# A recurrence in four chunks: the next chunk's inverse moved between this chunk's state products, with second buffers and banks of their own

## The reference

```
def step(state, inp):
    r_t, w_t, k_t, v_t, a_t, b_t = inp
    sa = jnp.einsum('bhvk,bhk->bhv', state, a_t)
    state = (state * w_t[:, :, None, :] + sa[..., None] * b_t[:, :, None, :]
             + v_t[..., None] * k_t[:, :, None, :])
    return state, jnp.einsum('bhvk,bhk->bhv', state, r_t)
```

## Time and profile before

| | |
|---|---|
| runs | 2697.29, 2707.37, 2708.58 us; median 2707.37 |
| profiled execution | 2712.13 us, of which the span of the instructions is 2710.4 |
| mean granted TensorE clock | 0.966 |
| recurrence, from 216.0 to 382.6 us | 166.6 us; TensorE busy 150.2, VectorE 66.5, ScalarE 35.4, clock 0.86 |

### The profile page before, as it was taken

How to read it: one execution, slowest core, us unless ns; L and a number is a source line. 1 busy time by engine, 2 the same in 40 slices (tenths; PEclk the granted TensorE clock), 3 DMA queues, 4 the chain that set the end, 5 groups by cost and what they waited for, 6 DMA issues and landing times.

```text
span 2710.4 us, 29623 instructions
## 1 busy us (share of the span) xinstructions
PE 2567.2 (95%) x12176; PEld 1986.1 (73%) x12176; DVE 1481.6 (55%) x1678; ACT 1133.3 (42%) x1329; POOL 155.1 (6%) x185
## 2 busy tenths in 40 slices
PE   6989989799999999899989999999999899999998
PEld 4667866587788887687757768888868566888876
DVE  3675343788888888546565543333354744333344
ACT  3422222577787777322334232222252644222223
POOL 1000001111110110000000100000100010000010
PEclk9888889899999999999989999999999999999999
DMA  6122321599999999422201222232312012222220
GB/s 255 61 77 103 110 78 62 209 359 366 362 357 359 360 354 341 160 79 97 86 20 63 80 84 84 80 109 76 118 63 93 32 43 75 80 99 105 69 99 31
DMA packets 64569, 388.77 MB, mean 143 GB/s; under 512 B 13361, under 2 KB 13489, under 8 KB 22577
## 3 DMA queue, kind: packets, MB, share of 16 engines
q1 hardware_dynamic: 53712, 373.20, 38.2%
q0 software_dynamic: 9280, 8.42, 0.9%
q10 hardware_dynamic: 1440, 5.24, 0.5%
HBM read 391.00 MB, written 20.97 MB: 152 GB/s over the span
## 4 chain that ended last, share of the span: by engine, by line
PE 81%; DVE 8%; ACT 4%; DMA 3%; issue 2%; POOL 0%; DVEq 0%; ACTq 0%; SPq 0%; POOLq 0%
PE psD L2696 67%; DMA ring<-w_moe 3%; PE psA L1984 1%; PE psA L2769 1%; DVE ring_r L935 1%; PE psA L2924 1%; DVE ring_r L2379 1%; ACT ring_r L2197 1%; ACT ring_r L733 1%; PE psA L2914 1%; PE psA L1054 1%; PE psD L1928 1%; PE psA L2015 1%; PE psA L2704 1%; PE psA L2749 1%
## 5 line engine op out<-in xcount | busy, mean ns | idle before, releaser
L2696 PE MATMUL psD<-rounded,ring_r 128*128 128x512 f32 (+1 forms) x6168 | 1454.9, 397 | 16.4 <-DVE ring_r L2379 12.6
L2696 PEld LDWEIGHTS psD<-rounded,ring_r 128*128 128x128 f32 (+1 forms) x6168 | 1155.6, 188 | 316.2 <-issue 22.5
L2379 DVE TENSOR_TENSOR ring_r<-ring,ring_r 128x2048 fp32r<-128x2048 f32 (+3 forms) x143 | 307.0, 2147 | 235.7 <-ACT ring_r L2197 232.0
L2696 PE MATMUL psD<-ring_r,rounded 128*128 128x512 f32 (+1 forms) x1728 | 411.0, 394 | 7.4 <-DVE ring_r L935 2.8
L2197 ACT ACTIVATE ring_r<-ring 128x2048 fp32r<-128x2048 f32 (+3 forms) x143 | 251.9, 1762 | 390.4 <-PE psD L2696 370.2
L2696 PEld LDWEIGHTS psD<-ring_r,rounded 128*128 128x128 f32 x1728 | 318.3, 190 | 89.1 <-issue 9.7
L935 DVE TENSOR_TENSOR ring_r<-ring,ring_r 128x2048 fp32r<-128x2048 f32 x128 | 293.1, 2291 | 47.2 <-ACT ring_r L733 45.9
L733 ACT ACTIVATE ring_r<-ring 128x2048 fp32r<-128x2048 f32 x128 | 245.2, 1917 | 59.3 <-DMA ring<-w_moe 33.2
L2696 PE MATMUL psD<-rounded,rounded 128*128 128x512 f32 x768 | 191.9, 398 | 0.3 <-DVE rounded L935 0.3
L1761 DVE TENSOR_TENSOR arena<-arena,psD 128x512 f32<-128x512 f32 x44 | 30.2, 686 | 254.9 <-ACT arena L1456 254.9
L2696 PEld LDWEIGHTS psD<-rounded,rounded 128*128 128x128 f32 x768 | 139.5, 188 | 27.9 <-issue 0.7
(11 more groups left out here) (406 smaller groups left out, 2172.9 us busy)
## 6 DMA issues: line engine op xcount, KB each, us to landing
ring<-w_moe SPq DMA_DIRECT2D x192, 1024.0 KB, 7.2
ring<-w_dense SPq DMA_DIRECT2D x134, 1024.0 KB, 4.8
ring<-w_dense SPq DMA_DIRECT2D x16, 768.0 KB, 4.1
ring<-w_dense SPq DMA_DIRECT2D x16, 640.0 KB, 3.9
arena<-x_t SPq DMA_DIRECT2D x1, 2048.0 KB, 7.8
token_rows<-arena ACTq DMA_DIRECT2D x4, 512.0 KB, 2.6
arena<-pair_rows SPq DMA_DIRECT2D x4, 512.0 KB, 7.8
arena<-pair_rows ACTq DMA_DIRECT2D x4, 512.0 KB, 8.5
```

What stands on the lines that cost most here:

```text
L2379: dve.tensor_tensor(lo_, ring_of(u, nk, nco), hi, ALU.subtract).then_inc(sem("w_lo"), 1)
L2696: mm = pe.matmul(out, w[a], x[b], start=start and i == 0, stop=stop_ and i == 2)
```

## The change

The loop over chunks is taken apart. TensorE first does chunk 0's transposes, products and inverse. Then for d = 1 to 3 it interleaves the products and the inverse of chunk d with the state products of chunk d-1, and the state products of chunk 3 stand at the end. In detail:

- XT, AB and AK get a second buffer each for odd chunks, in slots of the weight ring that are idle at this time. GpSimd clears the second XT (128x1024) before it signals `consts` for chunk 0.
- `u0`, `sa`, `y` and `st` get the four banks of psD, one each, with counters `chain` and `chain_free`.
- The product `xn` is gone. VectorE transposes the new 32x32 blocks of `xt` from PSUM into XI (four instructions a chunk in place of two additions).
- `ab` and `ak` alternate between the two row halves of the array product by product, and VectorE masks two banks with one instruction.
- One `gm` in each chunk; its scratch moves to the mask area of levels 0 to 3, and GpSimd builds only levels 5 and 6.
- Some semaphores of other stages are merged under new names (`gains`, `prep`), with the same waits.

```diff
@@ aux_plan
+    a += tokens(0) + [("mr", 1, 0)] + four("ab", 0) + four("ak", 0) + [("gm", 0)]
+    a += two("u", 0, 5) + [("mr", 1, 1)] + two("xt", 0, 5) + [("mo", 0, 0)]
+    a += two("u", 0, 6) + [("mr", 1, 2)] + two("xt", 0, 6) + [("mr", 1, 3), ("mo", 0, 1)]
+    for d in range(1, NCH):
+        a += four("ab", d) + four("ak", d) + [("gm", d)] + tokens(d)
+        a += two("u", d, 5) + [("mr", d + 1, 0), ("mr", d + 1, 1)] + two("xt", d, 5) + [("mo", d, 0), ("mr", d + 1, 2)]
+        a += two("u", d, 6) + [("mr", d + 1, 3)] + two("xt", d, 6) + [("mo", d, 1)]
@@ build
+        XTS = [flat(25600, 1024), ring[:, g1_at + UNIT:g1_at + UNIT + 1024]]
+        CHAIN = ("u0", "sa", "y", "st")
+        def chain_at(name):
+            i = CHAIN.index(name)
+            return psD[:, i // 2, i % 2, :]
@@ gpsimd
-            for i, m in enumerate(level):
-                b = 1 << i
+            for i in (5, 6):
+                m, b = level[i], 1 << i
...
-            pool.memset(flat(24576, 2048), 0.0).then_inc(sem("consts"), 1)
+            step(pool.memset(flat(24576, 2048), 0.0))
+            pool.memset(XTS[1], 0.0).then_inc(sem("consts"), 1)
@@ scalar
+            for d in range(NCH + 1):
+                if d < NCH:
+                    diagonals(d)
+                if d > 0:
+                    c = d - 1
+                    chain_copy("u0", c, UU, chain_at("u0"))
+                    chain_copy("sa", c, SAS, chain_at("sa"))
+                    chain_copy("y", c, V[:, :, P * c:P * c + P], chain_at("y").rearrange("p (j t) -> p j t", j=4))
+                if d == NCH:
+                    break
+                by_tokens(d)
...
@@ vector
+            def masked(nm, d, q, ops):
+                ready(dve, (nm, d, q + 1))
+                v = two_banks((nm, d, q))
+                for ins in ops(v):
+                    step(ins)
...
+            def level_5(d):
                 for q in range(2):
                     qs = slice(512 * q, 512 * q + 512)
-                    for nm, buf in (("xn", XI), ("xt", XT)):
-                        n_ = (nm, c, 5, q)
-                        ready(dve, n_)
-                        take(n_, dve.tensor_tensor(buf[:, qs], buf[:, qs], bank(n_), ALU.add))
+                    n_ = ("xt", d, 5, q)
+                    ready(dve, n_)
+                    v = bank(n_).rearrange("p (h t) -> p h t", h=4)
+                    xi = XI[:, qs].rearrange("p (h t) -> p h t", h=4)
+                    for lo_ in (0, 64):
+                        step(dve.transpose(xi[lo_ + 32:lo_ + 64, :, lo_:lo_ + 32],
+                                           v[lo_:lo_ + 32, :, lo_ + 32:lo_ + 64]))
                     dve.nop().then_inc(sem("x_new"), 1)
+                    take(n_, dve.tensor_tensor(XTS[d % 2][:, qs], XTS[d % 2][:, qs], bank(n_), ALU.add))
+            for d in range(NCH):
+                diagonals(d)
+                ab_masks(d)
+                ak_masks(d)
+                mixed(d)
+                if d > 0:
+                    new_state(d - 1)
+                level_5(d)
+                columns(d, 0)
+                level_6(d)
+                columns(d, 1)
@@ tensor
+            def products(nm, src, d):
+                tk = slice(P * d, P * d + P)
+                for q in (0, 2):
+                    outs = [aux((nm, d, q + o_)) for o_ in range(2)]
+                    for i in range(2):
+                        j = q + i
+                        for o_ in range(2):
+                            hp = slice(HD * o_, HD * o_ + HD)
+                            mm = pe.matmul(outs[o_][:, 256 * i:256 * i + 256].rearrange("p (a t) -> p a t", a=2),
+                                           src[hp, j, tk], AR[hp, j, d, :, :], start=True, stop=True)
+                            if i == 1:
+                                filled(mm)
...
+            by_tokens(0)
+            modulation(1, 0, 8)
+            products("ab", A, 0)
+            products("ak", K, 0)
+            mix_tokens(0)
+            half(5, 0)
+            modulation(1, 1, 9)
+            whole(5, 0)
+            to_column(("mo", 0, 0), MROW, 4, ("mr", 1, 1))
+            half(6, 0)
+            modulation(1, 2, 10)
+            whole(6, 0)
+            modulation(1, 3, 11)
+            to_column(("mo", 0, 1), MROW, 4, ("mr", 1, 3))
...
+            for d in range(1, NCH):
+                products("ab", A, d)
+                u0(d - 1)
+                sa(d - 1)
+                products("ak", K, d)
+                y(d - 1)
+                mix_tokens(d)
+                st(d - 1)
+                by_tokens(d)
+                half(5, d)
+                modulation(d + 1, 0, 8 + 4 * d)
+                modulation(d + 1, 1, 9 + 4 * d)
+                whole(5, d)
+                to_column(("mo", d, 0), MROW, 4, ("mr", d + 1, 1))
+                modulation(d + 1, 2, 10 + 4 * d)
+                half(6, d)
+                modulation(d + 1, 3, 11 + 4 * d)
+                whole(6, d)
+                to_column(("mo", d, 1), MROW, 4, ("mr", d + 1, 3))
+            u0(NCH - 1)
+            sa(NCH - 1)
+            y(NCH - 1)
+            chain_freed(pe, "y", NCH - 1)
```

More of the change, by code:

```diff
@@ new lines, in by_tokens, with halfway @@
+            def by_tokens(d):
+                for nm, buf in (("vt", VTK), ("bt", BTK), ("kt", KTK)):
+                    ready(act, (nm, d))
+                    if d > 0:
+                        chain_ready(act, "st", d - 1)
+                    act.activation(buf, bank((nm, d)), ACT.Copy).then_inc(freed((nm, d)), 1)
+            def halfway(d, lv):
+                for q in range(2):
+                    ready(act, ("u", d, lv, q))
+                    act.activation(UI[:, 512 * q:512 * q + 512], bank(("u", d, lv, q)), ACT.Copy)\
+                       .then_inc(freed(("u", d, lv, q)), 1)
@@ L2566, in columns, with diagonals @@
                    .then_inc(freed(n_), 1)
-            for c in range(NCH):
-                dve.wait_ge(sem("consts"), c + 3)
+            def diagonals(d):
+                dve.wait_ge(sem("consts"), d + 3)
                 for b in range(4):
[L2571 to L2574, removed]
-                    ready(dve, n_)
[L2576 to L2583, removed]
-                dve.nop().then_inc(sem("lm"), 1)
[L2585 to L2590, removed]
@@ L2623, in _, with new_state @@
-                columns(c, 1)
-            for c in range(NCH):
-                dve.wait_ge(freed(("y", c)), AUX_NO[("y", c)] // 4 + 1)
+            def new_state(c):
+                chain_ready(dve, "st", c)
+                fac = gain[:, 32:48].rearrange("p (j c) -> p j c", c=4)[:, :, c:c + 1].to_broadcast([P, 4, P])
+                stv = ST.rearrange("p (j v) -> p j v", j=4)
+                t1v = T2[:, :].rearrange("p (j v) -> p j v", j=4)
+                psv = chain_at("st").rearrange("p (j v) -> p j v", j=4)
+                blkb = blk.unsqueeze(1).to_broadcast([P, 4, P])
+                dve.wait_ge(sem("chunk_gain"), 1)
+                step(dve.tensor_tensor(t1v, psv, blkb, ALU.mult))
+                if c > 0:
+                    step(dve.tensor_tensor(t1v, t1v, stv, ALU.add))
+                step(dve.tensor_tensor(stv, t1v, fac, ALU.mult))
+                dve.nop().then_inc(sem("state"), 1)
@@ L2918, in new @@
-                def new(nm, lv, q):
-                    n_ = ("u", c, lv, q)
-                    out = aux((nm, c, lv, q))
-                    pe.wait_ge(freed(n_), AUX_NO[n_] // 4 + 1)
-                    one, two = (XT, UI) if nm == "xn" else (UI, XT)
-                    for i in range(4):
-                        mm = pe.matmul(out[:, P * i:P * i + P], hs(one, 4 * q + i), hs(two, 4 * q + i),
-                                       start=True, stop=True)
-                    filled(mm)
-                pe.wait_ge(sem("lm"), c + 2)
@@ new lines, in half @@
+            def half(lv, d):
+                if lv == 5:
+                    pe.wait_ge(sem("lm"), d + 2)
+                for q in range(2):
+                    out = aux(("u", d, lv, q))
+                    if lv == 6:
+                        pe.wait_ge(sem("x_new"), 4 * d + q + 1)
+                    for i in range(4):
+                        mm = pe.matmul(out[:, P * i:P * i + P], hs(LM[lv], 4 * q + i), hs(XI, 4 * q + i),
+                                       start=True, stop=True)
+                    filled(mm)
@@ new lines, in whole @@
+            def whole(lv, d):
+                if lv == 5:
+                    pe.wait_ge(sem("xt_in"), d + 1)
+                for q in range(2):
+                    n_, old = ("u", d, lv, q), ("xt", d, 5, q)
+                    out = aux(("xt", d, lv, q))
+                    pe.wait_ge(freed(n_), AUX_NO[n_] // 4 + 1)
+                    if lv == 6:
+                        pe.wait_ge(freed(old), AUX_NO[old] // 4 + 1)
+                    for i in range(4):
+                        mm = pe.matmul(out[:, P * i:P * i + P], hs(UI, 4 * q + i), hs(XTS[d % 2], 4 * q + i),
```

(2 more changed lines are left out.)

275 lines of the change are left out of this document (126 added, 149 removed).

## The result

| | before | changed |
|---|---|---|
| median of the runs, us | 2707.97 (2697.29 to 2709.58, 4 runs) | 2660.16 (2656.5 to 2666.41, 4 runs) |
| the same, measured again beside each other | 2704.29 (9 runs) | 2663.78 (2660.27 to 2665.52, 5 runs) |
| profiled execution | 2712.13 | 2666.41 |

The ratio is 0.9835, with a 95% interval of 0.9819 to 0.9851; measured again it is 0.9846 (0.9832 to 0.9859). So the change saves 40 to 48 us by the medians, and 38 to 49 by the two intervals. I had predicted 2667, that is 40.6 us less, with a range of 2653 to 2684.

What follows compares the result with a forecast made beforehand. TensorE was taken as the bound, slowed by mask waits and lower clock. Recurrence -38.1 and start -2.5 make -40.6: profiled 2712.1 gives 2671.5, and as that execution lies 4.8 above the median, 2667; range 2653 to 2684.

Steps and rivals of the forecast that it cites:

- Who sets the pace: Recurrence: TensorE sets the pace, mostly at full clock, 30.4 us a chunk if VectorE keeps up; chance 0.72.
- Chunk 1: Second chunk of the recurrence: 28.4 us, as 30.4 less a third of `y` and of `u0`, without state yet.
- Chunk 0: First chunk: `gm` at 226.4, lower clock in `gm`, half and modulation, then full pace; chunk 1's `ab` at 243.6.
- The end: After the last chunk: `u0`, `sa`, `y`, their waits and a copy, 10.0 us together.
- The stage in all: Recurrence, first transposes to mean products: ends at 344.3 against 382.45, so -38.1 us, with 1.5 counted for lower clock.
- The step "-2.5 us": Kernel's start: GpSimd's constants come earlier, weights become the limit, and column sums start at 18.0, not 20.53.
- A clock that falls in every chunk: Rival: lower clock in `u0`, a half and `y` of each chunk, as before; 14.7 us in three chunks, 2680; chance 0.15.
- VectorE as the bound: Rival: two-bank masks cost twice, or TensorE meets a bank not yet free; some 20 us in all, 2687; chance 0.06.

Runs made afterwards that it cites:

- `xn` back: Changed kernel with the `xn` product back and VectorE adding it to XI in place of the four transposes: 2670.05 us, 0.9875 of before.
- one-bank masks: Changed kernel with VectorE's masks on one PSUM bank each again: 2663.61 us, 0.985 of before.
- the sequence: Changed kernel's parts with the chunks in sequence again, as in the kernel before: 2688.15 us, 0.9939 of before.
- with dummies: Changed parts in sequence, plus never-read products on TensorE before each `ak` pair and before `u0`: 2679.95 us, 0.9901 of before.
- old order dummies: Kernel before, with small unused products where TensorE waits for masks, order of work unchanged: 2696.69 us, 0.9965 of before.
- the kernel with nothing else changed: Kernel before with only GpSimd's masks of levels 0 to 4 left out (the short start): 2705.13 us, 0.9998 of before.

## Why the prediction was right, and where it was off

**Who sets the pace.** Right. Chunks 2 and 3 last 29.9 and 29.8 us against 30.4 forecast. The step marks of VectorE came as laid out: masks done 6.6 us after `ab` (6.5), the first `ak` mask at 8.6 (8.6). `xn` back costs nearly its full price, and one-bank masks cost nothing in these chunks.

**Chunk 1.** 28.4 forecast, 29.6 measured. The difference is the spell of lower clock in `sa` and `ak`, some 0.5 and 1.1 us. I had put 1.5 for one such spell into the sum without a place, so the sum holds.

**Chunk 0.** 243.6 - 213.6 = 30.0 forecast from the transposes to chunk 1's `ab`, 243.73 - 214.31 = 29.4 measured. That the two agree is luck. My sum up to `gm` has a slip: 219.6 with 1.1, 4.3, 1.1 and 1.3 is 227.4, not 226.4. `gm` was due 12.8 us after the transposes (13.8 without the slip) and began at 229.29 - 214.31 = 15.0. I had the lower clock in the wrong place as well: `gm`, the half and the modulation ran at full pace, and `ab` and `ak` before them did not. So from `gm` on the chunk took 14.4 us where I had 17.2, and the errors cancel.

**The end.** 10.0 and 10.0. The stage in all: 130.7 forecast, 128.7 and 129.4 measured.

**The split of the gain.** Read as a chain of stages, 168.9 goes to 149.9 in the sequence, to 140.7 with dummies and to 128.7 interleaved: 19, 9 and 12 us. Of the 19, `xn` is 8. The other 11 (9 if the 2.2 us of wait ahead of the stage is counted) are the cheaper masks, which lie on the path there (8.4 us a chunk before, 6.8 after), one modulation beside the transposes and less time at the lower clock; I didn't separate these. The 9 are clock, and the 12 (14 with that wait counted) the order. In the old order dummies give 13 us of stage (11 with that wait counted), for there is more of the lower clock to win. The shares are not independent: hiding the waits is also most of what keeps the clock.

**The start.** The step "-2.5 us" came out in its mechanism: the first product waits for DMA, and the column sums start 1.8 us earlier in one profile and 3.1 in the kernel with nothing else changed. As a term of the final time it is not confirmed; the interval of that kernel allows -4 to +3. So the 2.5 us of my 40.6 that stood for the start were not found, and the stage gave 2 more than its 38.1. That the second measurement's 40.5 meets 40.6 so closely is in part this.

**The size.** The first measurement gave some 45 us by the ratio and 48 by the medians, more than 40.6. The stage explains 40.1, and the start at most 4. The second measurement gave 41. In the profiled execution of before the part behind the recurrence took 2328.0 us; in all other profiles, that of the old order with the short start among them (2318.7), it took 2319 to 2325. So the rest of the 46 us between the two profiles looks like scatter between executions and not like the change.

**The rivals.** A clock that falls in every chunk did not come: 1.00 in chunks 2 and 3 of the first profile. But single spells stay, in chunk 1 there and in chunks 1 and 3 of the second profile (0.94 and 0.95). VectorE as the bound did not come, but it is near: 0.8 to 1.6 us before the second `ak` pair. The rule from the Trainium skill, "TensorE: Matmul & The Clock Gate", section "A second HAM failure mode: psum-queue depth-cycling", that small idles between groups of matmuls make the clock swing, fits the old order, where dummies in the small waits won 9.5 us. In the new one 0.69 us of wait a chunk left the clock up in chunks 2 and 3 of one profile, and not in chunk 3 of the other; that this wait brings the spells is not shown.

## What to carry to other kernels

Lay the new order out as a timeline of each engine, with durations from rows at full clock, and mark when each buffer comes free: here it gave the length of a chunk at full clock to 0.6 us. Waits of a microsecond or less cost twice in this kernel, once as time and once as lower clock behind them, and dummies in the waits show how much is the second. Once TensorE sets the pace, a pass removed pays nearly in full. Where a product needs another engine's copy, put products that don't need it in between. Check the parts of a sum as well as the sum: chunk 0 came out right with two steps wrong.

## What was not expected of the hardware

- In the first 20 us the granted clock reads 1.00, yet 16 modulation records take 1.93 us where later ones take 1.07. The changed kernel's trace has no clock record before 21.0 us, so a 1.00 there is no measurement.
- One VectorE instruction that masks two PSUM banks pays nothing for the second bank: 0.69 for 512 elements per partition, as in one bank, and 1.23 for 1024, less than two of 0.69.
- Nearly the same code from the kernel's start to the recurrence took from 205.4 to 219.0 us in eleven profiles. A gain of 2 us there can't be read from a single profile.
